# First block's attention heads in pairs: probabilities scaled before they are turned, both heads weighed in one go, outputs split from the bank

## The reference

```python
def conformer_conv(conv_in, conv_w, conv_b, ln_g, ln_b, w_conv_out):
    a, gt = jnp.split(conv_in, 2, axis=-1)
    z = a * jax.nn.sigmoid(gt)
    ...  # causal depthwise convolution of 31 taps over 512 channels, then:
    z = layer_norm(z + conv_b, ln_g, ln_b)
    return jax.nn.silu(z) @ w_conv_out

def attend(args):            # for each block of 128 queries, 8 heads
    s = jnp.einsum("bqhd,bkhd->bhqk", qn_b, k_nope)
    s = s + jnp.einsum("bqhr,bkr->bhqk", qr_b, k_rope)
    s = jnp.where(mask[None, None], s, neg)        # causal
    p = jax.nn.softmax(s, axis=-1).astype(v.dtype)
    return jnp.einsum("bhqk,bkhd->bqhd", p, v)     # 64 columns a head
...
merged = gates[:, :, 0] * conv_out + gates[:, :, 1] * mla_out
h = h + merged @ w_out
```

## Time and profile before

| | |
|---|---|
| median of three runs | 1450.43 us (1449.04 to 1453.2) |
| the profiled execution | 1450.99 us, span of its instructions 1449.3 us |
| TensorE busy | 1404.5 us (97%) |
| VectorE busy | 810.4 us (56%) |
| ScalarE busy | 569.1 us (39%) |
| POOL busy | 102.0 us (7%) |
| granted TensorE clock, mean | 0.994 |

### The profile page before, as it was taken

How to read it: one execution, slowest core, us unless ns; L and a number is a source line. 1 busy time by engine, 2 the same in 40 slices (tenths; PEclk the granted TensorE clock), 3 DMA queues, 4 the chain that set the end, 5 groups by cost and what they waited for, 6 DMA issues and landing times.

```text
span 1449.3 us, 19726 instructions
## 1 busy us (share of the span) xinstructions
PE 1404.5 (97%) x6651; PEld 1136.4 (78%) x6651; DVE 810.4 (56%) x1299; ACT 569.1 (39%) x936; POOL 102.0 (7%) x83
## 2 busy tenths in 40 slices
PE   6999999899998999999999999999999999999997
PEld 5788878677886888888888777877778778778885
DVE  5538898775556544335445476554555465455552
ACT  5534434443544433114333355333333344343232
POOL 0000000101302000000013321000000000000001
PEclk9999999999999999999999999999999999999998
DMA  5323233214421333233333323222323313323331
GB/s 152 88 68 76 48 75 78 79 56 133 126 90 45 96 93 116 87 87 102 89 100 90 98 66 98 87 76 77 90 72 90 90 58 90 90 73 90 100 94 66
DMA packets 242782, 126.14 MB, mean 87 GB/s; under 512 B 17026, under 2 KB 241363, under 8 KB 242738
## 3 DMA queue, kind: packets, MB, share of 16 engines
q1 hardware_dynamic: 242162, 123.47, 29.7%
q10 hardware_dynamic: 576, 2.10, 0.4%
HBM read 123.45 MB, written 2.10 MB: 87 GB/s over the span
## 4 chain that ended last, share of the span: by engine, by line
PE 69%; issue 18%; DVE 4%; POOL 4%; ACT 2%; DMA 2%; ACTq 0%; POOLq 0%; DVEq 0%; SPq 0%
PE lin L571 20%; PE lin L575 20%; PE lin L574 20%; PE ob L1010 1%; DVE wl L1455 1%; POOL kt L546 1%; ACT wh L1076 1%; POOL logit L553 1%; PE sc L648 1%; PE sc L613 1%; POOL qt L546 1%; PE tr L660 1%; PE sc L971 1%; PE ob L674 1%; DMA raw<-in_w_xkv_dram 0%
## 5 line engine op out<-in xcount | busy, mean ns | idle before, releaser
L1455 DVE TENSOR_TENSOR wl<-raw,wh 128x1024 fp32r<-128x1024 f32 x238 | 291.0, 1232 | 207.0 <-ACT wh L1076 201.5
L571 PE MATMUL lin<-uh,wh 128*128 128x512 f32 x752 | 304.3, 405 | 5.2 <-DVE pt L1940 2.1
L575 PE MATMUL lin<-uh,wl 128*128 128x512 f32 x752 | 294.1, 391 | 0.0
L574 PE MATMUL lin<-ul,wh 128*128 128x512 f32 x752 | 293.7, 391 | 0.0
L1076 ACT ACTIVATE wh<-raw 128x1024 fp32r<-128x1024 f32 x238 | 238.6, 1011 | 123.0 <-DMA raw<-in_w_mlp_dram 43.3
L571 PE MATMUL lin<-vh,wh 128*128 128x512 f32 x576 | 232.4, 404 | 1.7 <-DVE pt L1940 0.8
L575 PE MATMUL lin<-vh,wl 128*128 128x512 f32 x576 | 225.2, 391 | 0.0
L574 PE MATMUL lin<-vl,wh 128*128 128x512 f32 x576 | 224.5, 390 | 0.0
L571 PEld LDWEIGHTS lin<-uh,wh 128*128 128x128 f32 x752 | 141.8, 189 | 40.0 <-issue 4.5
L574 PEld LDWEIGHTS lin<-ul,wh 128*128 128x128 f32 x752 | 142.0, 189 | 29.6 <-issue 2.6
L575 PEld LDWEIGHTS lin<-uh,wl 128*128 128x128 f32 x752 | 141.5, 188 | 30.2
(11 more groups left out here) (385 smaller groups left out, 1739.2 us busy)
## 6 DMA issues: line engine op xcount, KB each, us to landing
raw<-in_w_in_dram SPq DMA_DIRECT2D x101, 512.0 KB, 3.7
raw<-in_w_mlp_dram SPq DMA_DIRECT2D x64, 512.0 KB, 4.0
raw<-in_w_out_dram SPq DMA_DIRECT2D x16, 512.0 KB, 3.6
raw<-in_w_xkv_dram SPq DMA_DIRECT2D x8, 512.0 KB, 3.6
raw<-in_w_proj_b_dram SPq DMA_DIRECT2D x8, 512.0 KB, 3.5
raw<-in_w_proj_a_dram SPq DMA_DIRECT2D x8, 512.0 KB, 3.6
xtok<-in_x_dram ACTq DMA_DIRECT2D x4, 512.0 KB, 5.4
raw<-in_w_mla_out_dram SPq DMA_DIRECT2D x4, 512.0 KB, 3.6
```

The lines of the kernel that those rows point to most:

```text
L571: ins = pe.matmul(o, wh[:, slot, at], xh_, start=start, stop=False)
L574: pe.matmul(o, wh[:, slot, at], xl_, start=False, stop=False)
L575: return pe.matmul(o, wl[:, slot, at], xh_, start=False, stop=stop)
L1455: dve.tensor_tensor(wl[:, c.slot(4), 0:size], raw[:, c.slot(2), 0:size], wh[:, c.slot(4), 0:size].bitcast(F32), ALU.subtract).then_inc(lo_ ...
```

## The change

Two heads form a unit. In each head the exponentials are multiplied by the reciprocal of their sum (four activations with a scale, on ScalarE) before they are turned. The turned tiles go to the banks of the scores and from there to `pa`, `pb` and `pt`. The second head of a unit weighs the values of both: for each key block one matmul per head, with 64 columns of values as weights and the turned probabilities streamed through; the first head's go to partitions 0 to 63 of `ob`, the second's to 64 to 127. So the outputs come turned already, and ScalarE and VectorE split them from the bank once per unit. The sixteen transposes and the output multiplications are gone. The mean of the convolution moves into the first chunk of `mla_out`, the sum of squares from behind its first chunk to behind its second, the broadcast from behind the second into the middle of the third. The convolution's sums lie over tiles of its input that have been used up. The taps in the three runs of a head are 7, 3 and 6 instead of 6, 5 and 5.

```diff
+            def turn_rows(n, banks, rows):
+                for q in rows:
+                    wait(pe, probs_scaled, n.times(4, q + 1))
+                    for kb in range(q + 1):
+                        b, o = banks[kb]
+                        ins = pe.transpose(b[:, o + (q - kb) * P:o + (q - kb + 1) * P],
+                                           logit[:, LOFF[q] + kb * P:LOFF[q] + (kb + 1) * P], ident[:])
+                if QT - 1 in rows:
+                    ins.then_inc(turned_ready, 1)
+            def weigh_both(n1, weights):
+                wait(pe, turned_act, n1.times(1, 1))
+                wait(pe, turned_dve, n1.times(1, 1))
+                for kb in range(QT):
+                    for p in range(2):
+                        rows = slice(64 * p, 64 * p + 64)
+                        ins = pe.matmul(ob[rows, kb * P:S], vtok[:, kb, rows], weights[p][kb], start=kb == 0,
+                                        stop=kb == QT - 1)
+                ins.then_inc(ob_ready, 1)
...
-                job(c + 2, j + 2, DT, uh, ul, between={3: turn_values_and_score})
-                job(c + 3, j + 3, DT, uh, ul,
-                    between={3: first_part, 4: parts[1], 5: parts[2], 7: parts[3]})
-                parts[4]()
-
-
-            pe.wait_ge(conv_added, CT - 1)
-            pe.matmul(sc[0][:], ones[:], conv_total[:], start=True, stop=True).then_inc(mean_ready, 1)
-            pe.wait_ge(out_copied, HEADS + 1)
-            for f in range(4):
-                if f >= 2:
-                    pe.wait_ge(o_low, f - 1)
-                turn_tile(sc[1 + f % 2], lambda q: otok[:, q, f * P:(f + 1) * P]).then_inc(ot_ready, 1)
+                between = {1: turn_first, 3: lambda: turn_rows(n, TURNED[1], (3,))}
+                if p:
+                    between[7] = lambda: weigh_both(n, FIRST_WEIGHTS)
+                job(c + 2, j + 2, DT, uh, ul, between={2: score, 5: turn_values})
+                job(c + 3, j + 3, DT, uh, ul, between=between)
...
-                two_jobs(c + m, j + 2 * m, oh, ol, tiles_of(o_low, 0) if m == 0 else None)
-                if m == 0:
+                two_jobs(c + m, j + 2 * m, oh, ol, tiles_of(o_low, 0) if m == 0 else None,
+                         {0: sum_conv, 2: lambda: broadcast("conv")}.get(m))
+                if m == 1:
                     sum_total("conv")
-                if m == 1:
-                    broadcast("conv")
...
                 exps(n)
+                split(c + 4)
+                wait(act, rden_made, n.times(1, 1))
+                for q in range(QT):
+                    at = logit[:, LOFF[q]:LOFF[q] + KEYS[q]]
+                    act.activation(at, at, ACT.Copy, scale=rden[:, q:q + 1]).then_inc(probs_scaled, 1)
                 to(j + 2, gates[:, g, :], ACT.Tanh, scale=0.5)
-                split(c + 4)
                 split(c + 5)
-                copy_turned(n, 0)
-                copy_turned(n, 1)
+                wait(act, turned_ready, n.times(1, 1))
+                act.activation(FIRST_WEIGHTS[p][0], sc[0][:], ACT.Copy)
+                act.activation(FIRST_WEIGHTS[p][1], sc[1][:, 0:384], ACT.Copy).then_inc(turned_act, 1)
                 split(c + 6)
...
+                maxima(n)
                 wait(dve, vtr_ready, n.times(1, 1))
-                dve.tensor_copy(vtok[:, :, 0:VD], ob[:, 256:512].rearrange("p (q d) -> p q d", q=QT))\
-                    .then_inc(vtok_placed, 1)
-                maxima(n)
+                dve.tensor_copy(vtok[:, :, VD * p:VD * p + VD],
+                                tr[0][:, 0:QT * VD].rearrange("p (q d) -> p q d", q=QT)).then_inc(vtok_placed, 1)
+                run(1)
+                wait(dve, probs_made, n.times(4, 4))
+                dve.reciprocal(rden, den).then_inc(rden_made, 1)
                 lower(c + 4)
                 lower(c + 5)
-                run(1)
-                middle(n)
                 run(2)
-                at = n.times(VD)
-                outputs(n, otok[:, :, at:at + VD] if n.i is None else otok[:, :, bass.ds(at, VD)])
+                wait(dve, turned_ready, n.times(1, 1))
+                at = (pa[:, 896:1280], pb[:])[p]
+                dve.tensor_copy(at, sc[2][:, 0:384]).then_inc(turned_dve, 1)
                 lower(c + 6)
...
-                for p, cuts in ((0, (0, 6, 11, 16)), (1, (16, 22, 27, TAPS + 1))):
-                    head(c + 4 * p, j + 4 * p, n + p, lambda k: [tap(w) for w in range(cuts[k], cuts[k + 1])])
+                for p, cuts in ((0, (0, 7, 10, 16)), (1, (16, 23, 26, TAPS + 1))):
+                    head(c + 4 * p, j + 4 * p, n + p, p, lambda k: [tap(w) for w in range(cuts[k], cuts[k + 1])])
+                low(ol[:, t, :], ob[:], oh[:, t, :], o_high, (Idx(t) if isinstance(t, int) else Idx(0, 1, t)).times(1, 1),
+                    o_low)
```

More of the change, by code:

```diff
@@ L592, in job, with two_jobs @@
                 ins.then_inc(lin_ready, 1)
-            def two_jobs(c, j, xh_, xl_, before=None):
+            def two_jobs(c, j, xh_, xl_, before=None, between=None):
                 wait(pe, lo_made, (c + 1).v())
                 for m in range(2):
+                    if m and between is not None:
+                        between()
                     o = open_job(j + m)[:]
@@ L663, in scores_of_two @@
                             ins.then_inc(ready, 1)
[L665 to L676, removed]
@@ L999, in mix @@
                     ins.then_inc(mix_ready, 1)
-                job(c + 6, j + 6, DT, vh, vl, between={2: lambda: turn_rows(1, (0, 1, 2)), 4: lambda: turn_rows(1, (3,)),
-                                                       6: mix})
-                def weigh_both():
-                    wait(pe, turned_act, g.times(2, 2))
-                    wait(pe, turned_dve, g.times(2, 2))
-                    for kb in range(QT):
-                        for p in range(2):
-                            rows = slice(64 * p, 64 * p + 64)
-                            ins = pe.matmul(ob[rows, kb * P:S], vtok[:, kb, rows], WEIGHTS[p][kb], start=kb == 0,
-                                            stop=kb == QT - 1)
-                    ins.then_inc(ob_ready, 1)
-                job(c + 7, j + 7, DT, vh, vl, between={1: weigh_both})
+                job(c + 6, j + 6, DT, vh, vl, between={
+                    2: lambda: turn_rows(n1, TURNED[1], (0, 1, 2)), 4: lambda: turn_rows(n1, TURNED[1], (3,)), 6: mix})
+                job(c + 7, j + 7, DT, vh, vl, between={1: lambda: weigh_both(n1, WEIGHTS)})
                 pe.wait_ge(mix_read, g.times(1, 2))
@@ L1679, in _, with mla_out @@
             two_heads(c + 8 * (CT - 1), j + 8 * (CT - 1), CT - 1, Idx(2 * (CT - 1)))
+            c, j = phase("mla_out")
+            def mla_out(f):
+                g = gates[:, DT + f, :]
+                freed(dve.scalar_tensor_tensor(g, g, 1.0, read(j + f)[:], ALU.add, ALU.mult), j + f)
+            mla_out(0)
             dve.wait_ge(mean_ready, 1)
```

168 lines of the change are left out of this document (64 added, 104 removed).

## The result

| | before | changed |
|---|---|---|
| median, first comparison (8 and 8 runs) | 1450.8 us | 1457.45 us |
| ratio, 95% interval | | 1.0046 (1.003 to 1.0062) |
| second comparison, ratio | | 1.0049 (1.0032 to 1.0067) |
| the profiled execution, span | 1449.3 us | 1456.6 us |
| TensorE busy | 1404.5 us | 1403.1 us |

The change makes the kernel 0.46% slower, some 6.6 us on the medians. The forecast was 4.2 us; the time lies inside its range, above its middle.

What follows compares the result with a forecast made beforehand. TensorE, at work for 97% of the span, was taken as the bound. Pairs with the old tail +1.6, output projection +1.8 and setting in again +0.8 gave +4.2 us, 1454.6 us; eight-in-ten range 1450.5 to 1458.8.

Steps and rivals of the forecast that it cites:

- The chain of a head: In each head: maxima, exponentials, reciprocal, four scalings, then turns; even heads end at T+19.6 us, odd ones at T+23.8.
- The scalings' wait: In every head TensorE waits 1.1 to 1.3 us for the scaled tiles before its first transposes.
- The pairs: Pairs of heads take 43.4 us against 41.0 to 41.4, the last 44.9 against 50.1; together +1.6 us.
- setting in again: After a wait TensorE's next product costs about 0.1 us more; for the turns of eight heads +0.8 us.
- The tail: Output projection and normalised branch: broadcast waits 1.7 us, next stage's fourth tile starts at 29.6 us instead of 27.8; +1.8 us.
- The scaling's price: ScalarE's scalings cost what exponentials do, 0.71 us for 512 columns; at a plain tanh's 0.60 the sum is 2.9 us lower.
- The new places in memory: In the heads, the tensors' new places in memory cost nothing, since no instruction gets longer by them.
- Rivals 2 and 3: 2: VectorE falls behind, 1458.6 us, chance 0.10; 3: halves serial, 1463, or POOL's addition catches copy, 1457.9, 0.05 together.
- From there on both orders are the same, tile by tile: From the fourth tile of the stage after the output projection, both kernels run alike; no term was added for later stages.
- case 1: In the heads, the chain sets the pace as worked out: 1454.6 us, own range 1451.5 to 1457.5, chance 0.74.
- The rival on the other side: In the heads TensorE never waits for the chain: pairs of 39.7 us, -12.9 us in all; 0.06 including a half-way case.

Runs made afterwards that it cites:

- the four moves: Changed kernel with six taps before the maxima, four in VectorE's idle place, turns after three and four tiles, weighing after the last tile: ratio 0.9927 to before.
- before, again: The kernel before, unchanged, measured once more: median 1453.49 us, ratio 1.0001.
- wlate: Changed kernel with the weighing of both heads moved after the last tile of the odd head's gates job: ratio 1.0026 to the kernel before.

## Why the prediction was right, point by point

- **The chain of a head** was worked out to within 0.2 us. For the head that begins at T = 168.24 the reciprocal ends at T+12.8 (said: 12.9), the products go on at T+14.5 (14.65), VectorE idles for 2.47 us (2.4), its copy ends at T+20.6 (20.6), the weighing waits 1.46 us (1.5), and the next head begins at T+23.9 (23.8). Even heads take 19.6 (19.6), the last odd one 25.3 (25.3). The scalings' wait, said to be 1.1 to 1.3 us in every head, is 1.0, half of it between the transposes. *Right.*
- **The pairs.** Forecast +2.4, +2.4, +2.0 and -5.2; from the rows 44.32 - 41.44 = +2.9, 43.50 - 40.94 = +2.6, 43.46 - 41.48 = +2.0 and 44.83 - 50.07 = -5.2, with the distances before taken from first product to first product (104.07, 145.51, 186.45, 227.93, 278.00). That is +2.2, where 1.6 and the 0.8 for setting in again make 2.4. *Right.*
- **The tail.** 50.72 us to `w_out` instead of 327.06 - 278.00 = 49.06: +1.7, forecast +1.8; the wait for the diagonal was 1.3 instead of 1.7. *Right.*
- **The scaling's price**, chosen between two rows 2.9 us apart: the dearer one held, 2.8 us apart by the run without the factor. *Right.*
- **The new places in memory** made no instruction of the heads longer. Rivals 2 and 3 fell: TensorE waited for `qt` 0.3 us in all, and the halves overlap.
- **"From there on both orders are the same, tile by tile"** is the step that failed. The orders are the same, but the time of one stage, that with the memory's keys, is not: a term of +1.0 us (29.72 against 28.71 in traces without a slow stretch there) to +2.8 (32.1 against 29.35 in traces with one) was missing, which the shifted instruction fetch accounts for at least in part. With it the sum is 3.8 + 1.0 to 2.8, or 4.8 to 6.6, where executions at the same clock give 6.1. The rest of the 7.3 us between the two profiled spans is chance in the slow stretches. The forecast of +4.2 us was thus right for the stretch that the change touches and a third too low for the whole; that the median of 1457.45 us still lies inside the range, and barely inside the 1451.5 to 1457.5 of case 1, is owed to a width that was given for other terms.
- **The rival on the other side** (1437.5, if TensorE never waits) was worked out at 12.9 us under the kernel before; with the four moves the stretch from the first head to `w_out` is 222.99 - 211.07 = 11.9 us under, the whole 9.8; between the two lies the missing term of the point above.

## What to carry to other kernels

Follow the chain through one unit from row to row before looking at what the unit saves: here some 1.3 us saved in a pair met 3.8 us of waits (43.5 against 39.7), and the idle 2.4 us of VectorE in front of a split was both the cause of the wait in front of the weighing and the place for its cure. Move work of an in-order engine into its idle place before touching TensorE's order, and do not gather several short waits of TensorE into one long one. A stage that waits for loads can move by a microsecond or two when the code ahead of it changes its length, as it did here. Compare executions at the same granted clock before giving a cause to a difference under half a per cent.

## What the runs showed of the hardware

- A granted clock of 0.5 comes in stretches that lose 1.7 us of full speed each, or 3.4. They come after TensorE had waited for part of the time (it was at work for 1.5 to 3.2 us of the 4 ahead of those shown), and not always at the same places in two executions of the same code (450 to 454 us in one trace of the changed kernel, 405 to 409 in the other). The mean clock goes with most of the spread between executions (1446 to 1457 us of span for the kernel before, at mean clocks of 0.998 to 0.988).
- In the stage that waits for loads such a stretch cost the kernel before 0.6 us (29.35 against 28.71). With the new code the traces with one are 2.2 to 2.6 us longer there than those without (31.9 to 32.3 against 29.7 to 29.8); why is open. In full work it cost 1.5: from the first product with `fh` to the first with `vh` 315.0 us with one (before, again) and 313.5 without (wlate).
- A 16 KB packet on the instruction queue beside a weight chunk of 512 KB came with that chunk being 1.0 to 2.4 us late, its last packets trickling in at 20 GB/s. Where the packet came just as a chunk had landed, or between two, no chunk was late.
